# Two layers written out one behind the other, last sums and stores by tiles, and products that nobody reads in TensorE's waits

## The reference

```
# first block: routing of 256 tokens over 16 experts
probs = softmax(h @ w_router + b_router); pick a group, then the two best experts of it
y = sum over the two experts of weight * (silu(xb @ w_g[e]) * (xb @ w_u[e])) @ w_d[e]

# second block, for each of two layers
h   = rms_norm(x, norm_mix)
mem = rms_norm(mem_2, norm_mem)            # keys and values of the memory
... index branch, memory attention, own attention over 8 heads, delta-rule branch
x   = x + merged branches @ w_out
h   = rms_norm(x, norm_ffn)
x   = x + (silu(h @ w_gate) * (h @ w_up)) @ w_down      # 2816 wide, 22 chunks of 128
# behind the last layer
out = rms_norm(x, norm_final)
```

## Time and profile before

| | |
|---|---|
| median of 3 runs | 2700.69 us (2695.44 to 2703.59) |
| the profiled execution | 2700.96 us, of which 2699.1 us are its span |
| mean granted TensorE clock | 0.984 of full |
| PE busy | 2580.8 us, 96% of the span |
| DVE, ACT, POOL busy | 1887.9, 1511.8, 181.7 us |

### The profile page before, as it was taken

One profiled execution on the slowest core, in us unless ns is written; L12 is line 12 of the kernel. 1 busy time (PEld: TensorE's weight loads), 2 busy tenths in 40 slices (PEclk: granted clock), 3 DMA queues, 4 the chain that ended last, 5 costly groups with the idle time before them and its releaser, 6 DMA issues.

```text
span 2699.1 us, 44061 instructions
## 1 busy us (share of the span) xinstructions
PE 2580.8 (96%) x16251; PEld 2173.3 (81%) x16251; DVE 1887.9 (70%) x2149; ACT 1511.8 (56%) x1543; POOL 181.7 (7%) x211
## 2 busy tenths in 40 slices
PE   5999998999999999999999999999999999999997
PEld 3756887878787878879897787899898977878995
DVE  3444767999999999975677575555456785756553
ACT  4433555888888888863556453443345564533432
POOL 0000010000000000000074000000000740000000
PEclk9999998999999999999999999999999999999999
DMA  7434636999999999964433025454544340254545
GB/s 284 161 151 157 225 141 256 400 413 407 408 411 405 411 403 413 403 275 169 156 144 138 34 102 203 172 188 160 193 171 146 140 152 34 102 203 172 188 156 195
DMA packets 79658, 610.09 MB, mean 226 GB/s; under 512 B 16004, under 2 KB 21700, under 8 KB 24968
## 3 DMA queue, kind: packets, MB, share of 16 engines
q1 hardware_dynamic: 79496, 607.87, 58.3%
HBM read 606.79 MB, written 1.05 MB: 225 GB/s over the span
## 4 chain that ended last, share of the span: by engine, by line
issue 48%; PE 33%; DVE 8%; POOL 6%; DMA 2%; ACT 2%; SPq 1%; DVEq 0%; POOLq 0%; ACTq 0%
PE psum_scalar L1801 4%; PE psum_scalar L1802 4%; DVE weight_slabs_rounded L1759 3%; PE psum_vector L550 3%; PE psum_vector L552 3%; PE psum_vector L551 3%; POOL arena L3543 3%; PE psum_scalar L550 2%; PE psum_scalar L551 2%; PE psum_scalar L552 2%; POOL arena L3546 2%; DVE arena_rounded L1759 2%; PE psum_vector L1773 2%; DMA weight_slabs<-in_mixer_slabs 1%; PE psum_scalar L1841 1%
## 5 line engine op out<-in xcount | busy, mean ns | idle before, releaser
L2202 DVE TENSOR_TENSOR weight_slabs_rounded<-weight_slabs,arena_rounded 128x2048 fp32r<-128x2048 f32 x208 | 477.9, 2307 | 342.5 <-ACT arena_rounded L2199 293.2
L2199 ACT ACTIVATE arena_rounded<-weight_slabs 128x2048 fp32r<-128x2048 f32 x208 | 396.4, 1913 | 361.6 <-PE psum_vector L552 223.5
L550 PE MATMUL psum_scalar<-arena_rounded,arena_rounded 128*128 128x256 f32 (+1 forms) x1456 | 472.6, 325 | 20.1 <-DVEq L1294 7.5
L550 PE MATMUL psum_vector<-arena_rounded,arena_rounded 128*128 128x512 f32 (+3 forms) x1264 | 456.2, 361 | 15.0 <-DVE weight_slabs_rounded L2202 14.9
L1759 DVE TENSOR_TENSOR weight_slabs_rounded<-weight_slabs,arena_rounded 128x2048 fp32r<-128x2048 f32 x192 | 430.9, 2285 | 9.0 <-DVE arena L1978 3.9
L1747 ACT ACTIVATE arena_rounded<-weight_slabs 128x2048 fp32r<-128x2048 f32 x192 | 362.2, 1910 | 38.5 <-PE psum_scalar L1802 19.8
L552 PE MATMUL psum_vector<-arena_rounded,arena_rounded 128*128 128x512 f32 (+1 forms) x896 | 348.0, 388 | 0.0
L551 PE MATMUL psum_vector<-weight_slabs_rounded,arena_rounded 128*128 128x512 f32 x880 | 343.8, 391 | 0.0
L550 PEld LDWEIGHTS psum_scalar<-arena_rounded,arena_rounded 128*128 128x128 f32 x1456 | 278.7, 191 | 52.4 <-issue 22.3
L1801 PE MATMUL psum_scalar<-arena_rounded,arena_rounded 128*128 128x512 f32 x768 | 307.9, 401 | 2.7
L550 PEld LDWEIGHTS psum_vector<-arena_rounded,arena_rounded 128*128 128x128 f32 (+2 forms) x1264 | 237.9, 188 | 54.6 <-DVE weight_slabs_rounded L2202 11.5
(11 more groups left out here) (497 smaller groups left out, 4138.8 us busy)
## 6 DMA issues: line engine op xcount, KB each, us to landing
weight_slabs<-in_layer_slabs SPq DMA_DIRECT2D x103, 2048.0 KB, 7.7
weight_slabs<-in_expert_slabs SPq DMA_DIRECT2D x192, 1024.0 KB, 8.2
arena<-in_expert_slabs SPq DMA_DIRECT2D x96, 1024.0 KB, 8.5
weight_slabs<-in_mixer_slabs SPq DMA_DIRECT2D x32, 2048.0 KB, 8.3
weight_slabs<-in_layer_slabs SPq DMA_DIRECT2D x6, 1024.0 KB, 5.5
arena<-in_mem SPq DMA_DIRECT2D x3, 1024.0 KB, 11.9
arena<-in_b_gate SPq DMA_DIRECT2D x6, 512.0 KB, 8.3
arena<-in_x SPq DMA_DIRECT2D x1, 1024.0 KB, 5.2
```

The source lines that it names most:

```text
L550: pe.matmul(out, left[0], right[0], start=start, stop=False)
L2199: e.activation(fr(high), low, ACT.Copy).then_inc(S("weights_high"), 1)
L2202: e.tensor_tensor(fr(low), low, fr(high).bitcast(F32), ALU.subtract).then_inc(S("weights_split"), 1)
```

## The change

The loops over the two layers become Python loops, so that each engine has the second layer's instructions behind the first's and waits on constants. What prepared a third layer goes. The last pair of chunks of the product with `w_down` is made tile by tile; in layer 1 the sums, squares, final scaling and stores go tile by tile too, and `nfin` is loaded in the place of the memory rows of layer 1. `idle_products` makes products into a bank that nobody reads: 8 before the wait for routing, 2 and 1 in own attention (g = 0 and 1), 4 before the wait of the second norm.

```diff
+        def idle_products(pe, n):
+            for _ in range(n):
+                pe.matmul(pst[:, :], ident, cst[:, 0:BANK], start=True, stop=True)
...
+            idle_products(pe, 8)
             pe.wait_ge(S("routing"), 1)
...
-        nfin = room(72, D)
+        nfin = room(96, D)
...
-            with pe.Fori(0, 2) as l:          # so for all five engines
+            for l in range(2):
...
-                    if n == LS - 2:
+                    if n == LS - 2 and l == 0:
                         next_layer(0)
...
-                        sp.dma_start(mem_rows, ...)
-                next_layer(1)
-                next_layer(2)
-            sp.wait_ge(S("layer_free"), 3)
-            sp.dma_start(nfin, ...)
-            sp.wait_ge(S("layer_free"), 4)
-            sp.dma_start(out.rearrange("(t p) d -> p t d", p=P), x)
+                        if l == 0:
+                            sp.dma_start(mem_rows, ...)
+                        else:
+                            sp.dma_start(nfin, ...)
+                if l == 0:
+                    next_layer(1)
+                    next_layer(2)
+            for t in range(NT):
+                sp.wait_ge(S("layer_free"), 3 + t)
+                sp.dma_start(out[t * P:(t + 1) * P, :], x[:, t, :])
...
+                    idle_products(pe, 2 - g)
                     probs_to_T(at)
                     probs_to_T(at + 1)
...
+                idle_products(pe, 4)
                 pe.wait_ge(S("diagonals_ready"), 2 * l + 2)
...
-                    if n == 3:
+                    if n == 3 and l == 0:
                         memory_to_T(0)
-                    if n == 4:
+                    if n == 4 and l == 0:
                         memory_to_T(4)
...
-                for k in range(FC):
-                    for t in range(NT):
+                for pair in range(0, FC, 2):
+                    rows_first = pair == FC - 2
+                    for k, t in [(pair + (i % 2 if rows_first else i // 2),
+                                  i // 2 if rows_first else i % 2) for i in range(4)]:
...
-                Splitter(e, l + 1, high=True).upto(1)
+                if l == 0:
+                    Splitter(e, 1, high=True).upto(1)
...
-            e.wait_ge(S("x_ready"), 7)
-            squares(pre, x, xsq)
+            for t in range(NT):
+                e.wait_ge(S("x_ready"), 7 + t)
+                pre.go(e.activation(xsq[:, t, :], x[:, t, :], ACT.Square, accum_out=ss[:, t:t + 1]))
...
-                if n == 2:
+                if n == 2 and l == 0:
                     over_rms(mem_rows, mem_rows, 3, 5, "memn_ready")
-                if n in (3, 4):
+                if n in (3, 4) and l == 0:
                     memory_gains(4 * (n - 3))
...
             for t in range(NT):
-                pre.go(stt(x[:, t, :], x[:, t, :], rstd[:, t:t + 1], nfin, ALU.mult, ALU.mult))
-            pre.sync()
-            e.sem_inc(S("layer_free"), 1)
+                stt(x[:, t, :], x[:, t, :], rstd[:, t:t + 1], nfin, ALU.mult, ALU.mult).then_inc(S("layer_free"), 1)
```

More of the change, by code:

```diff
@@ L2167, in half_spent @@
         def half_spent(e, l, g):
[L2170 to L2173 removed]
+            name, value = lay_spent[LH * l + g]
+            e.wait_ge(parts["lay"][name], value)
         class Splitter:
@@ L2196, in upto @@
                         before = half_before(g)
-                        if before is not None and (before >= 0 or not isinstance(self.l, int)):
+                        if before is not None and LH * self.l + before >= 0:
                             half_spent(e, self.l, before)
@@ L2225, in sp_layers @@
                 load(n, 0)
-            with sp.Fori(0, 2) as l:
+            for l in range(2):
                 def vector(name, lo, hi):
@@ L2760, in pe_layers @@
                     project_T(V, hT)
-                    if n == 3:
-                        pe.wait_ge(S("memn_ready"), l + 2)
+                    if n == 3 and l == 0:
+                        pe.wait_ge(S("memn_ready"), 2)
                         memory_to_T(0)
-                    if n == 4:
+                    if n == 4 and l == 0:
                         memory_to_T(4)
                 banks = []
-                for k in range(FC):
-                    if k % 4 == 0:
-                        pe.wait_ge(S("ff_split"), 6 * l + k // 4 + 1)
-                    if k % 2 == 0:
-                        w = half()
-                    for t in range(NT):
+                for pair in range(0, FC, 2):
+                    if pair % 4 == 0:
+                        pe.wait_ge(S("ff_split"), 6 * l + pair // 4 + 1)
+                    w = half()
+                    rows_first = pair == FC - 2
+                    for k, t in [(pair + (i % 2 if rows_first else i // 2), i // 2 if rows_first else i % 2) for i in range(4)]:
                         for side in range(2):
@@ L2795, in squares @@
                 e.sem_inc(S("squares"), 1)
-            with e.Fori(0, 2) as l:
+            for l in range(2):
                 A = Banks(e, psa, m["scalar_full"], m["scalar_free"], base=LAY_A * l, looped=True)
@@ L3075, in act_layers @@
                         feed_forward_high(n - 1)
-                    if n == 1:
-                        e.wait_ge(S("mem_in"), 16 * l + 32)
+                    if n == 1 and l == 0:
+                        e.wait_ge(S("mem_in"), 32)
                         squares(step, mem_rows, xsq)
@@ L3081, in act_layers @@
                 weights.until(52)
-                Splitter(e, l + 1, high=True).upto(1)
-                assert (A.n, step.n) == (LAY_A, LAY_ACT), (A.n, step.n)
-            e.wait_ge(S("x_ready"), 7)
-            squares(pre, x, xsq)
+                if l == 0:
+                    Splitter(e, 1, high=True).upto(1)
+                assert (A.n, step.n) == (LAY_A, LAY_ACT - 2 * l), (A.n, step.n)
+            for t in range(NT):
+                e.wait_ge(S("x_ready"), 7 + t)
+                pre.go(e.activation(xsq[:, t, :], x[:, t, :], ACT.Square, accum_out=ss[:, t:t + 1]))
+            pre.sync()
+            e.sem_inc(S("squares"), 1)
         def vec_layers(e, pre):
@@ L3510, in vec_layers @@
                         V.give(tt(x[:, t, cols], x[:, t, cols], V.take(), ALU.add))
-                V.given()
-                e.sem_inc(S("x_ready"), 1)
-                e.sem_inc(S("layer_free"), 1)
-                assert (V.n, step.n) == (LAY_V, LAY_DVE), (V.n, step.n)
-            e.wait_ge(S("squares"), ROOTS_SO_FAR + 7)
-            root(pre, ROOTS_SO_FAR + 10, 2, D)
+                    if l == 1:
+                        V.given()
+                        e.sem_inc(S("x_ready"), 1)
+                if l == 0:
+                    V.given()
+                    e.sem_inc(S("x_ready"), 1)
+                    e.sem_inc(S("layer_free"), 1)
+                assert V.n == LAY_V - 4 * l and (l == 1 or step.n == LAY_DVE), (V.n, step.n)
+            e.wait_ge(S("squares"), ROOTS_SO_FAR + 6)
+            root(pre, ROOTS_SO_FAR + 9, 2, D)
             e.wait_ge(S("final_gain_in"), 32)
             for t in range(NT):
-                pre.go(stt(x[:, t, :], x[:, t, :], rstd[:, t:t + 1], nfin, ALU.mult, ALU.mult))
-            pre.sync()
-            e.sem_inc(S("layer_free"), 1)
+                stt(x[:, t, :], x[:, t, :], rstd[:, t:t + 1], nfin, ALU.mult, ALU.mult).then_inc(S("layer_free"), 1)
         def pool_layers(e, pre):
@@ L3550, in pool_layers @@
                 power(step, rstd, ss, 2, ROOTS_SO_FAR + 4 + 5 * l)
-                power(step, rstd, ss, 2, ROOTS_SO_FAR + 5 + 5 * l)
-            power(pre, rstd, ss, 2, ROOTS_SO_FAR + 11)
+                if l == 0:
+                    power(step, rstd, ss, 2, ROOTS_SO_FAR + 5)
+            power(pre, rstd, ss, 2, ROOTS_SO_FAR + 10)
         block = ctx.enter_context(nc.Block())
```

30 lines of the change are left out of this document (14 added, 16 removed).

## The result

| | before | after |
|---|---|---|
| median of the runs first shown | 2698.66 us (4 runs) | 2668.71 us (2665.69 to 2677.25, 4 runs) |
| ratio, 95% interval | | 0.9891 [0.9868, 0.9913] |
| profiled execution, span | 2700.96, 2699.1 us | 2677.25, 2675.5 us |
| with the runs beside the experiments, median | 2699.5 us (67 runs) | 2667.7 us (9 runs) |

The change makes the kernel 30 us faster where the forecast had 21.

The account below looks back on a forecast made before the run. The prediction took TensorE, busy for 96% of the span, to bound the kernel. Its terms, -2.5 - 1.6 - 1.7 - 7.7 - 3.2 - 2.8 - 1.5 = -21.0, took 2700.96 to 2680.0 us, range 2672 to 2689.

Parts of the forecast that it names:

- Term 1, the jump: At the end of layer 0, PE's 2.44 us pause for the loop's jump back goes: -2.5 us.
- Term 1, the registers: In both layers, constant waits need no register operations; 8 such waits a layer at 0.1 us each: -1.6 us.
- Term 2: In layer 1, the memory rows' transposes for a third layer go from PE: -1.7 us.
- Term 3: Behind PE's last product, the end takes 9.0 us instead of 16.75: -7.7 us.
- Term 4: At the second norm, four products in the wait keep the clock full: -1.6 us a layer, -3.2 together.
- Term 5: In own attention, products in the wait keep the clock full; g = 1 loses 0.4 us: -1.4 a layer, -2.8.
- rival on transposes: In own attention, transposes let the clock fall despite the products: that term becomes +0.8, total 2683.6 us; chance 0.08.
- Term 6: In routing, eight products fill the wait; the clock falls a few microseconds later, returning where it does now: -1.5 us.
- likeliest case: Whole kernel: all terms hold, 2680.0 us, own range 2676 to 2684; chance 0.57.
- all rivals: Clock stays at routing (2675.1, chance 0.15), falls in layers (2686.8, 0.17), falls by transposes (2683.6, 0.08), slower code (2709, 0.03).
- rival "slower, since written-out code has to be fetched": Fetching PE's written-out layers eats the gain from 4 ns a pair, shows as slower, 2709, from 5.6; chance 0.03.

Follow-up runs that it names:

- e5: The changed kernel with the layers' waits computed from a register on PE alone: 2678.56 us, ratio 0.9921.
- e10: The changed kernel with PE's waits computed from a register only in the delta-rule solve and around it: 2676.54 us, ratio 0.9919.
- e1: The kernel before with the two layers written out and constant waits, no added products, old end and third layer's preparation kept: 2690.76 us, ratio 0.9968.
- e4: The changed kernel run again, for its spread and a second profile: 2667.69 us, ratio 0.9887.
- e14: The changed kernel with the end of the kernel before put back: 2671.55 us, ratio 0.9893.
- e3: The changed kernel without any of the products that nobody reads: 2681.38 us, ratio 0.9938.
- e8: The changed kernel without the 4 products a layer ahead of the second norm: 2676.4 us, ratio 0.9911.
- e18: The changed kernel with layer waits from registers on PE, VectorE, ScalarE and GpSimd, and without any added product: ratio 0.9964.
- e7: The changed kernel without the 2 + 1 products a layer in own attention: 2671.52 us, ratio 0.9896.
- e9: The changed kernel without the 8 products in routing's wait: 2679.32 us, ratio 0.9926.
- e13: The kernel before with the added products alone; loops, third layer's preparation and end kept: 2694.9 us, ratio 0.9986.
- e15: The changed kernel plus products ahead of routing's second and third waits, the solve's second tile and (three a layer) the product with `w_down`: 2668.62 us, ratio 0.9885.
- e17: The kernel before with layers written out, constant waits and the added products; old end and third layer's preparation kept: ratio 0.9923.
- e11: The changed kernel plus 6 products that nobody reads ahead of the product with `w_down`: 2669.75 us, ratio 0.9885.
- e16: The changed kernel plus one product ahead of routing's second and third wait each: 2673.66 us, ratio 0.9906.

## Why the prediction was wrong, step by step

- **Term 1, the jump (-2.5): right.** The pause of 2.44 us is gone, and PE's starts move by 2.50 us at that place.
- **Term 1, the registers (-1.6): wrong, the first step that failed.** "Nearly all run while PE still works on queued products" is true of the long products, as far as the runs can tell, and false of the solve. Registers on PE cost 9.2 us (e5), nearly all of it in the solve and around it (e10); e1 leaves 8.6 - 2.5 = 6.1 us for them. The earlier trace rows showed the operations and their 32 ns; I counted only those behind a semaphore wait, and never asked where PE's sequencer had nothing in hand. The trace of before did show that: in its layer 0 solve PE pauses for 2.0 us, marked "issue". The bound, -4 for VectorE and ScalarE, looked at the wrong engines; theirs is 1.9 us or nothing.
- **Term 2 (-1.7): right.** The stage from layer 1's second norm to its last product is 195.3 us before and 193.5 in e4, with the same 3.4 us at half clock: -1.8.
- **Term 3 (-7.7): right in size.** 16.8 became 8.8 us where I had 9.0. Terms 2 and 3 together, 9.4 forecast, measure 8.1 and 9.7 us. Most of it is the third layer's doing and not the new order's (e14), a split that I did not make.
- **Term 4 (-3.2): right by the two profiles, perhaps too small.** By the profiles of before and after it is 5.22 to 3.59 us twice, -3.3. But the profile of before has a short stretch at half clock there; e1, e3 and e8 have 6 to 7 us of it in layer 0, and over the five profiles without its products (before, e1, e3, e8, e18) the norm takes 5.2 to 6.5 us, 5.9 on average, which makes -4.6. Taken away alone it costs 6.5 us (e8), 6 either way, which doesn't tell 3.2 from more.
- **Term 5 (-2.8): the size fits, the mechanism isn't shown.** 1.7 and 0.9 us in g = 0, given back by 0.2 a layer in g = 1 where I had 0.4. (Both groups in full, from `norms_to_rows` on, give 1.8 and 1.5 us.) But layer 0 runs as fast there in e1, e3 and e18, and both layers do in e7, all without these products. With them none of the profiles has the half clock there; without them the profiles of five kernels have it in five of ten places. Nor do the runs bear out the rival on transposes: the clock was 1.00 behind this wait with the products and, in five places, without them.
- **Term 6 (-1.5): wrong, the second step that failed.** "I take it that the clock falls there, a few microseconds later than now, and comes back where it does now" was half true: it falls later (429.6 in e4, 435.7 in the first profile) and returns sooner, after 10.2 or 6.8 us, so routing alone gives 2 to 4 us. In the first profile it was also halved from 418.6 to 425.4, while the products began, and eight of them took 8.0 us instead of 6.9. Taken away alone its products cost 10.5 us (e9, 6 either way), most of it elsewhere, which no term had. The likeliest case and all rivals looked at each wait's own stretch, as if a stretch gone from one place left the others alone. That is the step: the products were priced where they stand, at 7.5 us, and are worth some 12 to 14.

Together: forecast 4.1 + 9.4 + 7.5 = 21.0; measured 8.6 (e1) + 8.1 (e1 to e3) + 13.8 (e3 to e4) = 30.5 us. The surplus is 4.5 from registers and 6.3 from the clock, less 1.3 at the end, each with its scatter. That the half clock falls from 91 to 50 us a run is shown, and that the products do most of it (88 to 47, e3 to e4). Where they win what their own places don't show is open. In single profiles stretches come and go hundreds of microseconds away from the product that was added (e13, e15, there behind a wait for split weights that has grown), but they also do between two executions of one kernel: the changed kernel has 3.4 us from 251.4 and 6.8 from 418.6 on in its first profile and neither in its second, both ahead of layer 0. Which of them a kernel brings and which an execution, nothing here tells. Nor is it settled why the loop kernel alone profits so little.

The rival "slower, since written-out code has to be fetched" did not happen: the page counts 103 packets of instructions for this queue after and 108 before. But pauses that look like its mechanism are there in both kernels, in the solve.

## What to carry to other kernels

Ask of each stretch not only whether the engine is busy but whether its sequencer is ahead: among long products a wait computed from a register cost nothing that could be told, in a run of products 24 ns apart each cost some 46 ns here, and pauses marked "issue" in the profile are the sign. Price a product that only holds the clock by runs of the whole kernel with and without it, not by the stretch behind its own wait; here three such places were forecast at 7.5 us and worth 12 to 14 together, but 3.8 in a kernel that differed in its loops. A stretch at half clock is a loss only as far as the engine is busy in it. And take more than one profile before an engine's clock is argued from it: one and the same kernel had 75.7 and 41.1 us at half clock, 10 us of time.

## What the runs showed of the hardware that was not expected

- PE was at clock 0.50 for 30.7 us (after) and 27.3 us (e14) without a pause, in the solve of layer 1 and just behind it, beside other profiles of the same or nearly the same kernel with none there. The layer's solve took 37.3 and 37.6 us instead of 27 to 31. PE had waited 1.2 and 1.5 us for VectorE just before the clock fell; in e4 and e17 it waited as long in the same place, and the clock stayed at 1.00.
- PE's instructions come in packets of 16 KB, about one every 5 us in the solve, and pauses of 0.2 to 1.6 us end 2.2 to 3.0 us after such a packet's start (98 pauses in twenty profiles).
- A single wait in the midst of long products can be followed by half clock: in e11, e13, e15 and e16 PE waits 2.0 to 2.1 us for VectorE's split weights ahead of layer 1's second norm, and 0.6 to 1.5 us after the wait ends the clock goes to 0.50 for 3.4 us. Before waits 1.0 us there, after 0.8 and e4 0.7, and they keep the clock. It isn't the wait's length alone: e3 and e1 wait 1.9 and 2.1 us at this place in layer 0 and keep it. With such a wait and stretch the stage takes 142.3 to 142.8 us instead of 139.3 to 140.1.
